# Sums of squares of keys and queries as rows of 512 tokens on four column groups, then turned, in a two-block network on one core

## What is computed

```python
def l2norm(t):
    return t * lax.rsqrt(jnp.sum(t * t, -1, keepdims=True) + L2_EPS)

qkv = causal_conv_silu(p[..., :GDN_QKV], conv_w)
q = l2norm(qkv[..., :GDN_KEY].reshape(B, T, GDN_HEADS, GDN_DK))
k = l2norm(qkv[..., GDN_KEY:2 * GDN_KEY].reshape(B, T, GDN_HEADS, GDN_DK))
v = qkv[..., 2 * GDN_KEY:].reshape(B, T, GDN_HEADS, GDN_DV)
o = gated_delta_rule(q, k, v, g, beta)
```

## Time and profile before

| | |
|---|---|
| time, median of 3 runs | 1273.28 us (1273.1 to 1273.43) |
| profiled execution | 1274.28 us, its span 1272.5 us |
| TensorE busy | 1212.9 us, 95% of the span |
| VectorE busy | 554.0 us, 44% |
| ScalarE busy | 511.6 us, 40% |
| GpSimd busy | 382.4 us, 30% |
| mean granted TensorE clock | 0.974 of full |

### The profile page before, as it was taken

How to read it: one execution, slowest core, us unless ns; L and a number is a source line. 1 busy time by engine, 2 the same in 40 slices (tenths; PEclk the granted TensorE clock), 3 DMA queues, 4 the chain that set the end, 5 groups by cost and what they waited for, 6 DMA issues and landing times. The chain is left out here.

```text
span 1272.5 us, 16359 instructions
## 1 busy us (share of the span) xinstructions
PE 1212.9 (95%) x6592; PEld 1017.5 (80%) x6592; DVE 554.0 (44%) x859; ACT 511.6 (40%) x653; POOL 382.4 (30%) x92
## 2 busy tenths in 40 slices
PE   5889999999999988999999999999999799999997
PEld 5568878888878876888789887888888568999876
DVE  1464434444622245557954357522200714443635
ACT  4255543544411145654343424654311443335531
POOL 0014434444434423322222110034444225223220
PEclk9889999999989998999999999999999799999999
DMA  9992232222312233314321212023332323222101
GB/s 352 386 320 99 95 100 73 93 98 99 118 76 94 97 99 103 96 34 133 91 75 34 66 34 99 1 66 100 104 110 96 103 66 99 67 68 67 67 1 66
DMA packets 108574, 128.72 MB, mean 101 GB/s; under 512 B 13275, under 2 KB 99041, under 8 KB 108385
## 3 DMA queue, kind: packets, MB, share of 16 engines
q1 hardware_dynamic: 103412, 120.69, 28.3%
q10 hardware_dynamic: 5101, 7.15, 1.6%
HBM read 122.58 MB, written 5.24 MB: 100 GB/s over the span
## 5 line engine op out<-in xcount | busy, mean ns | idle before, releaser
L364 POOL TENSOR_TENSOR wl<-raw,wh 128x2048 fp32r<-128x2048 f32 x80 | 373.6, 4670 | 860.4 <-ACT wh L391 860.4
L242 PE MATMUL ps<-xth,wh 128*128 128x512 f32 x800 | 320.6, 401 | 3.6 <-DVE xtl L978 2.7
L244 PE MATMUL ps<-xth,wl 128*128 128x512 f32 x800 | 313.1, 391 | 0.0
L243 PE MATMUL ps<-xtl,wh 128*128 128x512 f32 x800 | 312.5, 391 | 0.0
L391 ACT ACTIVATE wh<-raw 128x2048 fp32r<-128x2048 f32 x80 | 153.0, 1912 | 373.1 <-PE ps L244 373.1
L242 PEld LDWEIGHTS ps<-xth,wh 128*128 128x128 f32 x800 | 151.1, 189 | 36.1 <-issue 6.7
L244 PEld LDWEIGHTS ps<-xth,wl 128*128 128x128 f32 x800 | 150.7, 188 | 32.4
L243 PEld LDWEIGHTS ps<-xtl,wh 128*128 128x128 f32 x800 | 151.2, 189 | 29.3 <-issue 0.2
L242 PE MATMUL ps<-wh,xth 128*128 128x256 f32 (+1 forms) x304 | 92.7, 305 | 2.0 <-DVE xtl L871 2.0
L244 PE MATMUL ps<-wh,xtl 128*128 128x256 f32 (+1 forms) x304 | 91.8, 302 | 0.0
L243 PE MATMUL ps<-wl,xth 128*128 128x256 f32 (+1 forms) x304 | 91.7, 302 | 0.0
(11 more groups left out here) (288 smaller groups left out, 1745.7 us busy)
## 6 DMA issues: line engine op xcount, KB each, us to landing
ada<-in_ada_w SPq DMA_DIRECT2D x24, 1024.0 KB, 10.6
raw<-in_gdn_w_in SPq DMA_DIRECT2D x24, 1024.0 KB, 5.1
raw<-in_ffn_w_up SPq DMA_DIRECT2D x22, 1024.0 KB, 4.9
raw<-in_gla_w_in SPq DMA_DIRECT2D x12, 1024.0 KB, 5.0
raw<-in_ffn_w_down SPq DMA_DIRECT2D x11, 1024.0 KB, 4.8
raw<-in_gdn_w_out SPq DMA_DIRECT2D x8, 1024.0 KB, 4.9
raw<-in_gla_w_out SPq DMA_DIRECT2D x4, 1024.0 KB, 5.0
xres<-in_x SPq DMA_DIRECT2D x4, 512.0 KB, 4.9
```

The costliest lines, as they stand in the source:

```text
L242: nc.tensor.matmul(o, lh, rh, start=first, stop=False)
L243: nc.tensor.matmul(o, lh, rl, start=False, stop=False)
L244: return nc.tensor.matmul(o, ll, rh, start=False, stop=last)
L364: nc.gpsimd.tensor_tensor(wl[:, s, :], raw[:, s, :], wh[:, s, :].bitcast(f32), ALU.subtract)\
```

## The change

The squares become the moving operand. The stationary one is a window of 32 columns out of `one_col`, whose column 32 alone is ones, so that a product adds the squares of one head over the channels and writes them as a row of 512 tokens, at row j of one of four groups of 32 partitions of bank 6. `sums` runs three times instead of eight: for units 0 and 1, 2 and 3 (four products each) and 4 to 7 (eight). ScalarE copies the bank (`sums_copy`), TensorE turns it in four blocks (`turn_sums`), and VectorE picks the columns that it needs.

```diff
+    sum_rows = at("sum_rows", TMP + 4 * KB, [T])
+    one_col = at("one_col", TMP + 12 * KB + 512, [64])
...
+            nc.gpsimd.memset(one_col[:], 0.0).then_inc(S("prepared"), 1)
...
+            nc.gpsimd.memset(one_col[:, 32:33], 1.0).then_inc(S("prepared"), 1)
...
+            def sums_copy(n):
+                act.wait_ge(S("ss_mm"), 2 * n + 1)
+                nc.scalar.activation(sum_rows[:], ps[:, 6, :], ACT.Copy).then_inc(S("sums_copied"), 1)
...
             def sums(n):
-                pe.wait_ge(S("sq_done"), n + 1)
+                last = (2, 4, 8)[n] - 1
+                pe.wait_ge(S("sq_done"), last + 1)
+                pe.wait_ge(S("prepared"), 8)
...
-                for sub in range(2):
-                    for tt in range(TT):
-                        c = (n * 2 + sub) * TT + tt
-                        mm = X.matmul(ps[:, 6, c:c + 1], squares[:, n, sub, tok(tt)], ones[:, 0:1], start=True, stop=True)
+                first = (0, 2, 4)[n]
+                for u in range(first, last + 1):
+                    j = (u - first) // 2
+                    for sub in range(2):
+                        c = 2 * (u % 2) + sub
+                        mm = X.matmul(ps[32 * c:32 * c + 32, 6, :], one_col[:, 32 - j:64 - j], squares[:, u, sub, :],
+                                      start=(j == 0), stop=(u + 2 > last))
+                mm.then_inc(S("ss_mm"), 1)
+
+            def turn_sums(n):
+                pe.wait_ge(S("sums_copied"), n + 1)
+                for tt in range(TT):
+                    mm = turn(ps[:, 6, tok(tt)], sum_rows[:, tok(tt)])
                 mm.then_inc(S("ss_mm"), 1)
...
-            chunk(1, 1, (3, do(gc_row, 0)), (6, do(gc_row, 1)), end=[do(sums, 0)])
+            chunk(1, 1, (3, do(gc_row, 0)), (6, do(gc_row, 1)))
-            chunk(2, 1, (3, do(gc_row, 4)), (6, do(gc_row, 5)), end=[do(sums, 1)])
+            chunk(2, 1, (3, do(gc_row, 4)), (4, do(sums, 0)), (6, do(gc_row, 5)), end=[do(turn_sums, 0)])
...
-            chunk(4, 1, (3, do(sums, 3)), (6, do(keys_keys, 4)))
+            chunk(4, 1, (2, do(sums, 1)), (4, do(keys_keys, 4)), (6, do(turn_sums, 1)))
...
-            chunk(8, 1, (3, do(keys_queries, 2)), end=[do(sums, 7)])
+            chunk(8, 1, (3, do(keys_queries, 2)), end=[do(sums, 2)])
...
-            chunk(9, 1, (3, do(turn_values, 0, 1)), end=[do(keys_queries, 3)])
+            chunk(9, 1, (3, do(turn_values, 0, 1)), (6, do(turn_sums, 2)), end=[do(keys_queries, 3)])
```

More of the change, by code:

```diff
@@ L646, in _ @@
             first(2)
+            sums_copy(0)
             decay(0)
@@ L657, in _ @@
             first(4)
+            sums_copy(1)
             root(scal[:, RKI, :, 4:8])
@@ L665, in _ @@
             second(8)
+            sums_copy(2)
             first(9)
+            second(9)
             root(scal[:, QS].rearrange("p t h -> p (t h)"))
-            second(9)
             first(10)
@@ L1076, in key_sums, with query_sums @@
                 V.tensor_scalar(scal[:, RKI, :, 4 * half:4 * half + 4],
-                                ps[:, 6, 16 * half:16 * half + 16].rearrange("p (h t) -> p t h", t=TT), EPS, None, ALU.add)\
+                                ps[:, 6, :].rearrange("p (t c j) -> p t c j", c=4, j=32)[:, :, :, 0], EPS, None, ALU.add)\
+                    .then_inc(S("mean_done"), 1)
+            def query_sums():
+                v.wait_ge(S("ss_mm"), 6)
+                V.tensor_scalar(scal[:, QS].rearrange("p t (j c) -> p t j c", c=4),
+                                ps[:, 6, :].rearrange("p (t c j) -> p t j c", c=4, j=32)[:, :, 0:2, :], EPS, None, ALU.add)\
                     .then_inc(S("mean_done"), 1)
@@ L1124, in values @@
                 if h == 0:
[L1125 removed]
+                    v.wait_ge(S("ss_mm"), 5)
                 V.tensor_tensor(val[:, 2 * half:2 * half + 2, h, :], ps[:, 3, :].rearrange("p (t n) -> p t n", n=DV),
@@ L1184, in _ @@
             taps(1, 0)
-            v.wait_ge(S("mask_ready"), 1)
+            v.wait_ge(S("gates_ready"), 1)
             dec(0)
@@ L1198, in _ @@
             v.wait_ge(S("gc_exp"), 3)
-            v.wait_ge(S("beta_done"), 1)
+            v.wait_ge(S("gates_ready"), 2)
             key_factors(0)
@@ L1575, in _ @@
             pe.wait_ge(S("c_silu"), 1)
-            pe.wait_ge(S("prepared"), 6)
+            pe.wait_ge(S("prepared"), 7)
             pe.wait_ge(S("cols_done"), 4)
@@ L1741, in sums @@
             def sums(n):
-                pe.wait_ge(S("sq_done"), n + 1)
+                last = (2, 4, 8)[n] - 1
+                pe.wait_ge(S("sq_done"), last + 1)
+                pe.wait_ge(S("prepared"), 8)
                 if n == 0:
                     pe.wait_ge(S("glog_done"), 1)
-                if n in (2, 4):
-                    pe.wait_ge(S("mean_done"), 1 + 2 * TT + TT + n // 2)
-                for sub in range(2):
-                    for tt in range(TT):
-                        c = (n * 2 + sub) * TT + tt
-                        mm = X.matmul(ps[:, 6, c:c + 1], squares[:, n, sub, tok(tt)], ones[:, 0:1], start=True, stop=True)
+                else:
+                    pe.wait_ge(S("mean_done"), 1 + 2 * TT + TT + n)
+                first = (0, 2, 4)[n]
[10 more added lines that the diff above has]
+                    mm = turn(ps[:, 6, tok(tt)], sum_rows[:, tok(tt)])
                 mm.then_inc(S("ss_mm"), 1)
@@ L1909, in _ @@
             chunk(1, 0, (3, gate_sums))
-            chunk(1, 1, (3, do(gc_row, 0)), (6, do(gc_row, 1)), end=[do(sums, 0)])
+            chunk(1, 1, (3, do(gc_row, 0)), (6, do(gc_row, 1)))
             chunk(2, 0, (3, do(gc_row, 2)), (6, do(gc_row, 3)))
-            chunk(2, 1, (3, do(gc_row, 4)), (6, do(gc_row, 5)), end=[do(sums, 1)])
+            chunk(2, 1, (3, do(gc_row, 4)), (4, do(sums, 0)), (6, do(gc_row, 5)), end=[do(turn_sums, 0)])
             chunk(3, 0, (3, do(gc_row, 6)), (6, do(gc_row, 7)))
-            chunk(3, 1, (3, do(keys_keys, 0)), (6, do(keys_keys, 1)), end=[do(sums, 2)])
+            chunk(3, 1, (3, do(keys_keys, 0)), (6, do(keys_keys, 1)))
             chunk(4, 0, (3, do(keys_keys, 2)), (6, do(keys_keys, 3)))
-            chunk(4, 1, (3, do(sums, 3)), (6, do(keys_keys, 4)))
+            chunk(4, 1, (2, do(sums, 1)), (4, do(keys_keys, 4)), (6, do(turn_sums, 1)))
             chunk(5, 0, (3, do(keys_keys, 5)), (6, do(keys_keys, 6)))
-            chunk(5, 1, (3, do(keys_keys, 7)), end=[do(sums, 4)])
+            chunk(5, 1, (3, do(keys_keys, 7)))
             chunk(6, 0)
-            chunk(6, 1, end=[do(sums, 5)])
+            chunk(6, 1)
             chunk(7, 0)
-            chunk(7, 1, end=[do(sums, 6)])
+            chunk(7, 1)
             chunk(8, 0, (3, do(keys_queries, 0)), (6, do(keys_queries, 1)))
-            chunk(8, 1, (3, do(keys_queries, 2)), end=[do(sums, 7)])
+            chunk(8, 1, (3, do(keys_queries, 2)), end=[do(sums, 2)])
             chunk(9, 0, end=[do(turn_values, 0, 0)])
-            chunk(9, 1, (3, do(turn_values, 0, 1)), end=[do(keys_queries, 3)])
+            chunk(9, 1, (3, do(turn_values, 0, 1)), (6, do(turn_sums, 2)), end=[do(keys_queries, 3)])
             chunk(10, 0, (3, do(keys_queries, 4)), (6, do(turn_values, 1, 0)), end=[do(turn_values, 1, 1)])
```

11 lines of the change are left out of this document (5 added, 6 removed).

## The result

| | before | changed |
|---|---|---|
| median | 1273.36 us, 4 runs (1273.1 to 1274.21) | 1264.86 us, 4 runs (1264.46 to 1266.72) |
| profiled execution | 1274.28 us, span 1272.5 | 1264.94 us, span 1263.1 |
| granted clock, mean of the span | 0.974 | 0.976 |

The ratio is 0.9935, with a 95% interval of 0.9918 to 0.9952: the kernel became 8.5 us faster in this comparison. All medians, means and ranges of this document leave out three single executions of 1387, 1537 and 1546 us, at a mean granted clock of 0.75 to 0.84, which some later comparisons contain.

A forecast was written before the change was run, and what follows sets the result against it. TensorE was taken as the bound, with VectorE's never-idle inversion deciding up to the first turned values. 4.0 + 0.6 - 1.0 = 3.6 us off the median 1273.28 gave 1269.7 us, range 1266.0 to 1272.2.

The forecast's parts named there:

- the first stretch: Up to VectorE's inversion of the diagonal: four sums go, two sets and two turns come, TensorE 4.2 us earlier.
- the sum in unit 6: VectorE's last sum of a piece starts 0.07 us behind GpSimd and is held by the shared ports; 1.9 us lost.
- the block in unit 8: A VectorE product held 4.38 us until GpSimd's low part ends; GpSimd comes earlier, so it ends 1.7 us earlier.
- the first values: First turned values from VectorE's inversion, which TensorE waits for: 4.2 - 1.9 + 1.7 = 4.0 us earlier.
- the root: Root of the query sums, gone from ahead of second(9): TensorE's 0.60 us wait for a SiLU goes, 0.6 gained.
- TensorE's 8.8 us: TensorE's work saved by the new sums, 4.8 us for 13.6; half was to go into waits for VectorE.
- my rival at 1267.1: Unit 6's sum slips past GpSimd unheld: 6.2 us gained, 1267.1 us, chance 0.25.
- I take 1.0: Loss from the clock falling to half behind TensorE's new wait; bounds 0 and 2.95 us, 1.0 taken.
- I take 3.6 off the median of the three runs: Whole-kernel sum: 3.6 us gain subtracted from the earlier kernel's median of 1273.28, giving 1269.7 us.
- TensorE alone decides: Rival: VectorE finds the time and all of 8.8 us counts, 1264.5 us; chance 0.06.
- theory B: Follow-up forecast: places where the clock falls are drawn anew each execution, moving the span by up to 3 us.
- theory A's second mechanism: Follow-up forecast: the changed program's shifted times, rather than its two memsets, make the 4.6 us outside the changed stretch.

The follow-up runs named there:

- the filler: Changed kernel with two sets of old one-column products, 3.4 us, put back unread on TensorE behind chunks (6, 1) and (7, 1); median 1265.22 us, ratio 0.9942.
- the key sums only: Changed kernel with query sums back to one-column products at chunk ends, and query_sums and the root in their old places; median 1265.37 us, ratio 0.9949.
- the split: Changed kernel with one column of VectorE's inversion (j = 22) moved behind the taps of chunk (6, 1); median 1265.8 us, ratio 0.9953.
- The memsets: Kernel before plus only the new column's two memsets on GpSimd at the start; two sets of runs, medians 1273.84 and 1270.39 us, ratios 1.0014 and 0.9998.
- the root's move alone: Kernel before with only the root of the query sums moved behind second(9); median 1268.48 us, ratio 0.9977.

## Why the prediction was wrong

**What held.** The sizes of the new products and turns; the 4.2 us of the first stretch (4.12 measured); that the sum in unit 6 is held by GpSimd, though it comes only 0.06 us behind; that the block in unit 8 shrinks by 1.7 (1.6); the first values at 4.0 (4.13); the root at 0.6 (0.65 left for it in the changed kernel, 0.8 alone). By these steps the local gain is 4.6 us; 4.79 were measured, and the three profiles of each kernel repeat their stretch within 0.15 us. A smaller miss cost nothing: VectorE's second half of the key sums came 1.0 us earlier than the marker shift alone gives (554.88 for 557.98, less 2.11), not 1.5. Half of TensorE's 8.8 us did go into waits: the runs with the filler and with the key sums only both show it. The Trainium skill (SBUF — State Buffer; "SBUF: two separate sides") calls the ports an exclusive lock which the first to start keeps to its end; the sum of 4.77 us agrees with that, and a share of bandwidth, or a slip past GpSimd (my rival at 1267.1), does not.

**The first step that failed: "I take 1.0" for the clock.** The fall came as foreseen, behind the wait of 3.04 us. I had written that what falls between the two new waits costs nothing, and then took a middle value, because I couldn't say between which products it would fall. It fell there in the changed kernel, and taking it away (the filler) changed nothing: it cost 0. With the split it fell behind the second wait and cost 0.8. For the changed kernel the term was mis-sized by 1.0 us.

**The second, and larger: "I take 3.6 off the median of the three runs".** This took the remaining 1030 us for a constant, and the three runs, 1273.1 to 1273.43, for its value. They were not: the same kernel gives 1268.25 to 1275.01, with a mean of 1271.74. Of the 9.4 us between the two profiled spans, 4.6 lie in untouched instructions: 1.0 before the third low part, 1.1 at 346 to 374, 1.0 between 761 and 1035, and 1.5 near the end. In the last three the granted clock differs: 0.88 for 0.94 over 340 to 368, 0.81 for 0.85 over 990 to 1036, and 0.92 for 0.96 over the 44 us around the last pair. In the first it doesn't, it is 0.90 up to the first low part in both. TensorE waited there for transfers of `ada_w`, 4.4 us in three waits before and 2.8 in two in the changed kernel; whether that makes the 1.0 was not tested. The 1.5 can be read from the markers before

```profile
1191.14 4.52 POOL L364 TENSOR_TENSOR wl<-raw,wh 128x2048 fp32r<-128x2048 f32 x1 [10.47 <-ACT wh L391]
1234.31 4.62 POOL L364 TENSOR_TENSOR wl<-raw,wh 128x2048 fp32r<-128x2048 f32 x1 [38.65 <-ACT wh L391]
```

and in the changed kernel, 43.17 us against 41.68:

```profile
1183.27 4.53 POOL L369 TENSOR_TENSOR wl<-raw,wh 128x2048 fp32r<-128x2048 f32 x1 [10.47 <-ACT wh L396]
1224.95 4.61 POOL L369 TENSOR_TENSOR wl<-raw,wh 128x2048 fp32r<-128x2048 f32 x1 [37.16 <-ACT wh L396]
```

From the mean of before, my 4.6 us without the clock's term would have given 1267.1, and a range around it should have had some 2 us on either side for this alone. The forecast missed by 4.8 us in all: 1.0 is the clock's term, 0.2 the other terms of the stretch, 1.5 the base, 0.8 the distance of the four changed runs' median from the mean of all 17, and 1.3 the untouched remainder, which stays open below.

**The number of a rival, not its mechanism.** "TensorE alone decides" gave 1264.5, 0.4 from the median. The filler and the key sums alone contradict it: 3.4 us put back on TensorE cost nothing, and 5.0 taken off it brought nothing. That the time came out near it is luck: it is the sum of the local 4.8, of runs of before that lay 1.6 us above their mean, and of untouched code.

**What stays open.** The 1.3 us by which the whole difference exceeds the changed stretch. The memsets don't make it, and neither need the new products, since the root's move alone had 2.2 us of it. What draws the places of the falls stays open too. The three profiles of before agree within 0.11 us behind the third low part, but those of the changed kernel don't (the pair at 346 took 26.90, 25.32 and 26.85 us), and the two with only the memsets have 43.18 and 41.65 us near the end. So theory B holds for some places and some kernels and is not shown as a rule. Whether a shift of the program's times (theory A's second mechanism) makes the falls fewer, these runs don't settle.

## What to carry to other kernels

Compare two profiles by a fixed pair of instructions around the change before you explain the total: here such a pair repeated within 0.15 us, while the total moved by over 6 us in an unchanged kernel. A few runs that agree don't show the spread of a kernel; take as its base, and as the width of the range, what many runs give. And a fall of the clock is charged like any work: it cost nothing where another engine's chain ended later (1.7 us of lost work, 0 on the time), half of its size behind the last wait of the split kernel (0.8 of 1.6), and nearly all of it between 346 and 374 (28.03 for 25.32 us, 2.7 of 2.95). So ask where it falls before giving it a price.

## What the runs showed of the hardware that I had not expected

- A wait of nearly the same length at the same place (3.27 and 3.28 us) was followed by 5.9 us of work at 1.2 GHz in one execution and 3.4 us in another, and in a third the clock stayed at 2.4 GHz. Yet in three profiles of the kernel before, the pair of markers around it took 28.03, 27.92 and 27.98 us.
- The clock also fell without a wait: 0.79 over 8 us in which TensorE was busy throughout, 96 us behind its last idle time (the memsets' first profile).
- Useless products in place of a wait kept the clock at 1.00 and lowered the time of a stretch by 0.9 us (241.29 to 240.41).
- A start 0.06 us behind GpSimd cost a sum of 198 elements 4.4 us.
- Moving in and out of the products on 32 columns costs little: 1.85 us for sixteen passes on the four groups, four on each. Eight more passes cost 1.85 - 0.99 = 0.86, so two rounds of the four groups, 0.43 us each; four rounds are 1.72, and 0.13 are left.
